# Gate rows read from a DRAM scratch with a partition stride of zero, in place of identity products, in a hybrid attention, convolution and RWKV step

## The reference, cut to what matters

```
sh1, sc1, g1, sh2, sc2, g2 = ada_modulation(cvec, w_mod, b_mod)      # six vectors of length D per group
h = rmsnorm(x, n1) * (1.0 + sc1) + sh1
... h @ w_in -> attention heads | conv module | RWKV heads, concatenated -> y
x = x + g1 * (y @ w_out)
h2 = rmsnorm(x, n2) * (1.0 + sc2) + sh2
x = x + g2 * conv_ffn(h2, w_up, ..., w_down)
```

## Time and profile before

| what | value |
|---|---|
| median of 3 runs | 2368.49 us (2366.16 to 2369.99) |
| the profiled execution's own time | 2366.93 us |
| its span in the trace | 2365.1 us |
| PE busy | 2162.2 us, 91% of the span |
| DVE busy | 1139.4 us, 48% |
| ACT busy | 764.0 us, 32% |
| POOL busy | 94.4 us, 4% |
| HBM traffic | 338.75 MB, mean 143 GB/s |

### The profile page before, as it was taken

The page is one execution under the profiler, slowest core; times in us unless marked ns, Lnnn a source line. Parts: engine busy times, 40 slices in busy tenths (PEclk is TensorE's granted clock), DMA queues, the critical chain, the costliest instruction groups (busy, mean ns, idle before and its releaser), DMA issues.

```text
span 2365.1 us, 43621 instructions
## 1 busy us (share of the span) xinstructions
PE 2162.2 (91%) x19181; PEld 1934.3 (82%) x19181; DVE 1139.4 (48%) x2060; ACT 764.0 (32%) x1287; POOL 94.4 (4%) x140
## 2 busy tenths in 40 slices
PE   5699999999568888869979999999999999999997
PEld 2588888987347666659979999999999999887885
DVE  1332225553867787853355444443444444445445
ACT  2232222221534343423333333233332334333432
POOL 1000000002111111100000000000000000000000
PEclk8899999999769998989989999999999999999998
DMA  9978677666210010006443334333333345433441
GB/s 380 338 252 304 246 267 268 245 237 192 46 28 7 3 34 3 5 15 219 125 143 108 128 130 130 129 125 125 125 125 125 127 127 190 127 125 111 133 129 54
DMA packets 209741, 338.75 MB, mean 143 GB/s; under 512 B 9501, under 2 KB 169875, under 8 KB 207696
## 3 DMA queue, kind: packets, MB, share of 16 engines
q1 hardware_dynamic: 207712, 329.77, 41.3%
q0 software_dynamic: 1840, 6.20, 1.0%
HBM read 328.43 MB, written 10.28 MB: 143 GB/s over the span
## 4 chain that ended last, share of the span: by engine, by line
PE 82%; DVE 12%; DMA 2%; ACT 2%; issue 2%; POOL 0%; DVEq 0%; POOLq 0%; ACTq 0%
PE ps L641 23%; PE ps L643 23%; PE ps L642 23%; PE ps L675 3%; DMA ring<-in_w_mod_dram 1%; PE ps L833 1%; PE ps L827 1%; PE ps L823 1%; DVE arena L1719 1%; PE ps L1004 1%; DVE stat L1580 1%; PE ps L843 1%; PE ps L861 1%; DMA ring<-in_w_in_dram 0%; PE ps L862 0%
## 5 line engine op out<-in xcount | busy, mean ns | idle before, releaser
L1412 DVE TENSOR_TENSOR w_split<-ring,w_split 128x1024 fp32r<-128x1024 f32 (+1 forms) x392 | 475.7, 1219 | 787.8 <-ACT w_split L1111 787.3
L1111 ACT ACTIVATE w_split<-ring 128x1024 fp32r<-128x1024 f32 (+1 forms) x392 | 407.7, 1051 | 817.5 <-PE ps L643 604.6
L641 PE MATMUL ps<-h_split,w_split 128*128 128x384 f32 x1776 | 600.5, 338 | 20.7 <-DVE w_split L1412 16.7
L642 PE MATMUL ps<-h_split,w_split 128*128 128x384 f32 x1776 | 596.9, 336 | 0.0
L643 PE MATMUL ps<-h_split,w_split 128*128 128x384 f32 x1776 | 596.8, 336 | 0.0
L641 PEld LDWEIGHTS ps<-h_split,w_split 128*128 128x128 f32 x1776 | 336.3, 189 | 33.4 <-DVE w_split L1412 18.7
L642 PEld LDWEIGHTS ps<-h_split,w_split 128*128 128x128 f32 x1776 | 336.3, 189 | 0.0
L643 PEld LDWEIGHTS ps<-h_split,w_split 128*128 128x128 f32 x1776 | 336.0, 189 | 0.0
L641 PE MATMUL ps<-w_split,h_split 128*128 128x256 f32 x960 | 275.3, 287 | 8.9 <-DVE w_split L1412 8.9
L642 PE MATMUL ps<-w_split,h_split 128*128 128x256 f32 x960 | 272.3, 284 | 0.0
L643 PE MATMUL ps<-w_split,h_split 128*128 128x256 f32 x960 | 272.3, 284 | 0.0
(11 more groups left out here) (363 smaller groups left out, 2643.5 us busy)
## 6 DMA issues: line engine op xcount, KB each, us to landing
ring<-in_w_mod_dram SPq DMA_DIRECT2D x96, 1024.0 KB, 7.8
ring<-in_w_up_dram SPq DMA_DIRECT2D x88, 1024.0 KB, 5.1
ring<-in_w_in_dram SPq DMA_DIRECT2D x46, 1024.0 KB, 5.5
ring<-in_w_down_dram SPq DMA_DIRECT2D x44, 1024.0 KB, 5.3
ring<-in_w_out_dram SPq DMA_DIRECT2D x16, 1024.0 KB, 5.6
arena<-in_x_sample_dram SPq DMA_DIRECT2D x4, 1024.0 KB, 16.5
x_mid<-arena SPq DMA_DIRECT2D x1, 3072.0 KB, 10.2
h_f<-x_mid SPq DMA_DIRECT2D x1, 3072.0 KB, 10.3
```

The source lines that it names most:

```text
L641: mm(o_, lh, rh, start=start, stop=False)
L642: mm(o_, lh, rl, start=False, stop=False)
L1111: AC(wh[k % SPLITS][:, 0:width(n)], arrived(n), ACT.Copy).then_inc(s_hi, 1)
L1412: V.tensor_tensor(wl[k % SPLITS][:, 0:w], arrived(n), wh[k % SPLITS][:, 0:w].bitcast(F32), ALU.subtract).then_inc(s_lo, 1)
```

## The change

The gates are turned once by two transposes, written to a DRAM scratch `gate_rows` of [2 gates][2 groups][2048], and read back by one DMA per gate whose source repeats the same 4096 values for all 128 partitions (`[[0, P], [1, 2 * D]]`). The two `gate_rows` calls on PE and ACT's 16 copies are gone.

In the order of the program:

- PE, between its waits for `s_mcol` and `s_cbuf`: two transposes of 128x32 of `modcol` to PSUM bank 4.
- ACT, ahead of the square for the variance (`csq`): a wait for these and one copy of 32x256 to `grow`.
- POOL, behind its masks: a wait for `grow` and four DMAs of 16 rows of 128 values to `gate_rows`; behind `s_pvc` a wait that they have landed. ACT, DVE and SP get the same wait at places that come later than that.
- SP: one DMA of 128x4096 to `gb` behind the loads of `x2` in the output projection, one to `gb2` behind piece 8 of the down projection.
- DVE waits for these DMAs (`s_gb`, `s_gb2`) where it waited for ACT's copies. PE's wait for `s_gb2c` at the start of the second half becomes one for `s_uact`.

```
+        grow, o = carve(wmix, o, 2, P)
...
+        G_dram = nc.dram_tensor("gate_rows", [2, 2, D], F32, kind="Internal").ap()
...
@@ SP, output projection, behind the three loads of x2
+                    sp.wait_ge(s_G, 64)
+                    sp.dma_start(gb.rearrange("p g d -> p (g d)"), bass.AP(G_dram.tensor, 0, [[0, P], [1, 2 * D]])).then_inc(s_gb, 16)
@@ SP, down projection
+                    if q == 0 and g == RING + 4:
+                        sp.dma_start(gb2.rearrange("p g d -> p (g d)"), bass.AP(G_dram.tensor, 2 * D, [[0, P], [1, 2 * D]])).then_inc(s_gb2, 16)
@@ POOL
+            pool.wait_ge(s_grow, 1)
+            for i in range(2):
+                for g in range(2):
+                    pool.dma_start(G_dram[i, g].rearrange("(k p) -> k p", p=P), grow[g:2 * KT:2, i, :]).then_inc(s_G, 16)
             pool.wait_ge(s_pvc, len(ATT) // 2)
+            pool.wait_ge(s_G, 64)
@@ PE
             pe.wait_ge(s_mcol, N_MOD)
+            for i, c0 in enumerate((2 * KT, 5 * KT)):
+                last = tr(ps[0:2 * KT, 4, toks(i)], modcol[:, c0:c0 + KT, :].rearrange("p k g -> p (k g)"), ident)
+            last.then_inc(s_gT, 1)
             pe.wait_ge(s_cbuf, 1)
...
-            def gate_rows(col0, ready, read):
-                for n in range(8):
-                    g, q = n // 4, n % 4
-                    if n >= 2:
-                        pe.wait_ge(read, n - 1)
-                    for j in range(4):
-                        col = modcol[:, col0 + 4 * q + j, g:g + 1].broadcast_to([P, P])
-                        last = mm(ps[:, 6 + n % 2, toks(j)], col, ident, start=True, stop=True)
-                    last.then_inc(ready, 1)
...
-                if j == 0:
-                    gate_rows(2 * KT, s_gbp, s_gbc)
...
-                                pe.wait_ge(s_gb2c, 8)
+                                pe.wait_ge(s_uact, FT)
...
-                    if i == 3:
-                        pe.wait_ge(s_uact, FT)
-                        gate_rows(5 * KT, s_gb2p, s_gb2c)
@@ ACT
+            ac.wait_ge(s_gT, 1)
+            AC(grow[0:2 * KT, :, :], ps[0:2 * KT, 4, 0:2 * P].rearrange("p (i c) -> p i c", i=2), ACT.Copy).then_inc(s_grow, 1)
+
             ac.wait_ge(s_ccen, 1)
...
-                if n == P_OUT + 2 * PARTS:
-                    for m in range(8):
-                        ac.wait_ge(s_gbp, m + 1)
-                        AC(gb[:, m // 4, 512 * (m % 4):512 * (m % 4) + 512], ps[:, 6 + m % 2, :], ACT.Copy).then_inc(s_gbc, 1)
...
-                if i == 6:
-                    for n in range(8):
-                        ac.wait_ge(s_gb2p, n + 1)
-                        AC(gb2[:, n // 4, 512 * (n % 4):512 * (n % 4) + 512], ps[:, 6 + n % 2, :], ACT.Copy).then_inc(s_gb2c, 1)
@@ DVE
-                        dv.wait_ge(s_gbc, 8)
+                        dv.wait_ge(s_gb, 16)
...
-                    dv.wait_ge(s_gb2c, 8)
+                    dv.wait_ge(s_gb2, 16)
```

More of the change, by code:

```diff
@@ L294, in build @@
         ss, o = carve(wmix, 0, 4, TOK)
+        grow, o = carve(wmix, o, 2, P)
+        assert o <= 2 * PART
         m4c, o = carve(wmix, 5 * TOK, 2, 4, CHUNK)
@@ L404, in build @@
              "s_stT", "s_stc", "s_stout"))
-        s_x2, s_gbp, s_gbc, s_oc = sem("s_x2"), sem("s_gbp"), sem("s_gbc"), sem("s_oc")
+        s_x2, s_gT, s_grow, s_G, s_gb, s_oc = (sem(n) for n in ("s_x2", "s_gT", "s_grow", "s_G", "s_gb", "s_oc"))
         s_ssq2, s_xn2, s_xtp, s_xts, s_h2 = sem("s_ssq2"), sem("s_xn2"), sem("s_xtp"), sem("s_xts"), sem("s_h2")
-        s_gb2p, s_gb2c = sem("s_gb2p"), sem("s_gb2c")
+        s_gb2 = sem("s_gb2")
         s_uc, s_ucv, s_usg, s_uact = sem("s_uc"), sem("s_ucv"), sem("s_usg"), sem("s_uact")
@@ L1229, in _ @@
             ac.wait_ge(s_expb, 1)
+            ac.wait_ge(s_G, 64)
             ac.wait_ge(s_out, 32)
@@ L1614, in _ @@
             dv.wait_ge(s_cc, 2)
+            dv.wait_ge(s_G, 64)
             dv.wait_ge(s_out, 32)
```

## The result

| what | before | changed |
|---|---|---|
| median, same chip, 4 runs each | 2367.32 us (2365.01 to 2369.99) | 2354.07 us (2352.29 to 2358.11) |
| ratio | | 0.9946, 95% interval 0.9929 to 0.9963 |
| the profiled execution's own time | 2366.93 us | 2353.58 us |
| its span | 2365.1 us | 2351.8 us |

A forecast was written before the change was run, and what follows sets the result against it. PE (TensorE) alone was taken to bound both stages. Removals of 7.43 + 7.32 = 14.75 us, additions 0, took 2366.93 to 2352.2; 1.56 more for a median gave 2353.7 us, range 2350.5 to 2359.0.

The forecast's parts named there:

- PE bounds both stages: Output and down projection: PE alone is the limit, busy 120.90 of 122.80 and 104.00 of 104.00 us at clock 1.00.
- Removed, 7.43 + 7.32 us: PE's gate products in the output projection (7.43 us) and down projection (7.32 us) leave the chain of waits.
- waits for banks: At both gates: the trace's 7.43 and 7.32 us beyond the skill's 7.1 us each would be PE waiting for banks.
- PE moves up by all of it; the splits are there: Output projection: block 1's last split ended at 1090.14, its part is wanted at 1100.5, so splits do not hold PE up.
- `gb` takes 6 us and lands at 1088: SP's queue, output projection: the first read takes 6 us (range 5 to 10), lands at 1088, piece 4 at 1091; cost 0.
- The deadlines, 1100.7 and 1102.5: Output projection, before part 8: `gb` may land as late as about 1100.7, weight piece 4 is needed by 1102.5.
- Second read, cost 0: Down projection: `gb2` fits between two weight issues with its 6 us, is wanted some 37 parts later, and costs 0.
- The end of the input projection, 0 to 0.4 us: Before the convolution's mean: two transposes fit PE's gap; cost taken as 0, bound 0.4 us; a mean after 579.8 means wrong.
- The starts across the two places 0.12 and 0.24 apart, landmarks 7.4 earlier, the end 14.8 earlier: Signs of being right: PE starts 0.12 and 0.24 us apart, landmarks up to the down projection 7.4 us earlier, end 14.8.
- The forecast for a median: Whole kernel: 2353.7 us, 0.62% faster, starting from a median of the runs before of 2368.49 us.
- the sum of 14.75 us: Whole kernel: the two removals together take off 14.75 us, with everything added costing 0.
- Rival 3: PE moves up, but time comes back at a fixed point, such as between down projection halves: 2356 to 2362; chance 0.05.

The follow-up runs named there:

- two copies of the read: Changed kernel with SP moving `gb` twice, the second time after the first landed, and DVE waiting for both: 2354.61 us (one run).
- three copies: Changed kernel with SP moving `gb` three times, each after the last landed, and DVE waiting for all: 2361.32 us (one run).
- the change in its third run: The changed kernel run once more without an edit: 2357.56 us (6 runs), ratio 0.9947 to the kernel before.
- products back again: Repeat of the changed kernel with both `gate_rows` calls and ACT's 16 copies put back, all additions kept: 2366.73 us (one run).
- first only: Changed kernel with the second gate's 32 products and ACT's 8 copies to `gb2` put back: 2364.75 us, ratio 0.9974 to the kernel before.
- second only: Changed kernel with the first gate's 32 products and ACT's 8 copies to `gb` put back: 2363.08 us, ratio 0.9975 to the kernel before.

## Why the prediction was right, point by point

- *PE bounds both stages.* Right: after the change it is busy for 120.93 of 122.80 and 104.00 of 104.00 us, as before.
- *Removed, 7.43 + 7.32 us.* Right: 7.4 and 7.4 us in the first pair of profiles, and the same with either place alone and in two repeats of the change. The estimate by the pass prices of the Trainium skill (FP8 and Floating Point Precision, TensorE Precision Notes; TensorE: Matmul & The Clock Gate, Wait — 56ns, not 53.3ns?), 14.3 us, is 0.5 us short. The prediction put that down to waits for banks, and this is only in part so. In the trace of before the 64 records of a place start 0.112 us apart, 7.14 us, which agrees with the skill. Three times at each place, at every second bank, one distance is 0.06 us longer, 0.17 us together, for a reason that no row shows. Only at the first place is there a wait for ACT: the third bank starts at 1089.41, right behind the first copy (1088.78 + 0.58), about 0.1 us late.
- *PE moves up by all of it; the splits are there.* Right: with two copies of the read even, PE has no gap in the 45.00 us around blocks 1 and 2, and the changed kernel has none up to the output projection's last product.
- *`gb` takes 6 us and lands at 1088.* It landed at 1087.9, and piece 4 at 1090.9 as forecast, but by luck: the queue ahead was through at 1082.9 and not at 1081.6, although the stage began 0.7 us earlier than before, and the read then took 5.0 us and not 6. The two errors cancel.
- *The deadlines, 1100.7 and 1102.5.* The second, for piece 4, is right: 2.3 us of splitting ahead of part 8 gave 4.6 us of lateness with three copies, and PE waited 4.53. The first, for `gb`, was never the one that ended a wait; only that a landing at 1097.2 costs nothing is shown. DVE's residual began at 1089.40 in the changed kernel, 6.5 us earlier than 1095.88 where "some 5" stood, 0.7 of it from the earlier start of the stage, and nobody gained by it.
- *Second read, cost 0.* Right: 10.0 us to landing, PE 104.00 of 104.00.
- *The end of the input projection, 0 to 0.4 us.* Right: the gap went from 0.91 to 0.81 us, and the kernel with all additions and no removal came out at 0.9994. The mean started at 578.5, not later than 579.8.
- *The starts across the two places 0.12 and 0.24 apart, landmarks 7.4 earlier, the end 14.8 earlier.* The starts are right. The landmarks behind the first place came 8.1 us (the norm) and 7.8 us (the last write of the up projection) earlier, 7.4 and what was gained before the mean. The end was 13.3 us earlier. The missing 1.5 us are +1.9 between the halves, +0.5 in the stretches without an edit, and -0.9 before the mean.
- *The forecast for a median.* 2353.7 against 2354.07. The mechanism is right, but the closeness is luck: the kernel before had a median of 2367.32 in this set, 1.2 us below the 2368.49 that the forecast started from, and the medians' gain was 13.25 us, 1.5 us short of 14.75; the two misses cancel to 0.3. By the ratios the sum of 14.75 us measured as 12.6 to 13.0 us in three sets of runs (0.9946, 0.9945, 0.9947). 14.75 would be 0.9938, inside each interval, but all three lie on the same side of it. Rival 3 named the place, the pause between the halves, and its size fits: that stretch spreads over 1.9 us, all of it clock. The long stretch does not need the change, as the kernel before shows the same 181.4 us. If the change makes it more frequent, the group means above would put that at 0.8 us, not at 1.8. Whether the rest is chance or a tendency of the clock stays open.

## What to carry to other kernels

Work that an engine at 100% does only to lay data out (here 64 products that spread a vector over the partitions) can go to a DMA from a scratch in memory, if the scratch is written well ahead (here it had landed 465 us before the read) and the read has a slack that is worked out from what is queued behind it. That slack is worth a sum, and the experiment that delays the DMA until it hurts shows it. When a gain comes out short by a microsecond or two, cut both traces at common landmarks and profile the old kernel once more before explaining it: here the shortfall lay in a stretch that varies by as much on its own.

## What the runs showed of the hardware that was not expected

- **The clock's answer to a short pause is not fixed.** Nearly the same waits of PE at the same place, 3.39 and 0.74 us or 3.40 and 0.92, gave 0.89 or 0.77 of full clock in 15 us, with the same kernel, and 179.8 or 181.4 us for the half. A single wait of 2.0 us still gave 0.89. Taking the pause away altogether gave 1.00 and saved 7.8 us where the waits were 4.8.
- **A stretch of identical work spreads over 7.8 us.** RWKV runs at a mean clock of 0.87 to 0.88. Before, and the change in its third run:

```profile
579.40:1060.45 481.05, 370.38 (x7576) 286.86 (x7576) 353.88 (x970) 193.87 (x447) 79.59 (x113) 0.88 0.10 21
```

```profile
579.40:1066.15 486.75, 377.22 (x7576) 291.43 (x7576) 353.56 (x970) 194.05 (x448) 81.82 (x117) 0.87 0.10 21
```

  The same 7576 records took 6.8 us more of PE, at 0.87 in place of 0.88, where the stretch is 5.7 us longer. Over all 14 profiles the stretch goes with the time that the granted clock stood at its lower level in it: 106 us of it in the shortest (products back again, 479.0 us), 114 in the first profiles of before (481.1) and of the change (481.2), 131 in the three longest (486.7, 486.7 and 486.8: first only, second only, the change's third). So the spread goes with the clock and is no mark of one kernel; what sets the clock's course there is not shown. The medians of the changed kernel differ by 3.5 us between sets and those of before by 2.8, which is of this size; one profile per set cannot show that this is their cause. Ratios are therefore taken within a set only.
- **A source row read 128 times costs nothing extra.** 2 MiB took 5.0 us behind the piece ahead of it in the queue, as for distinct rows, at 376 and 378 GB/s.
